# A decode and prompt step with PEER experts on one core: U and V rows in one table, one gather of 8 KB a pick, the gate of each pick on ScalarE

## The chip, the cores and the metric

The kernel runs on one core of a Trainium2 chip. The metric is device time in microseconds of one execution. The engines are TensorE (PE), VectorE (DVE), ScalarE (ACT), GpSimd (POOL) and SyncE (SP); each takes its instructions in the order in which they were written. POOL issues the gathers, SP the other transfers, and all of them share 16 DMA engines. "PEld" is the loading of weights into PE.

## What is computed

One layer on 1024 prompt tokens and 8 sample tokens, width 1024, all in float32: attention in two parallel groups of heads, an output projection, and then PEER, a layer of 16384 experts. Each expert is one row of `peer_u` and one row of `peer_v`. Each token takes 8 heads x 16 = 128 experts:

```python
def peer_ffn(h, w_q, sub_keys, u, v):              # for blocks hc of 128 tokens
    q = (hc @ w_q).reshape(128, PEER_HEADS, 2, 128)
    sc = jnp.einsum('chpd,hpkd->chpk', q, sub_keys)
    s1, i1 = lax.top_k(sc[:, :, 0], 16)
    s2, i2 = lax.top_k(sc[:, :, 1], 16)
    cand = s1[..., :, None] + s2[..., None, :]     # 256 candidates a head
    top_s, pos = lax.top_k(cand, 16)
    eid = take(i1 * N_KEYS + i2, pos)
    gate = jax.nn.softmax(top_s, axis=-1)
    act = jax.nn.gelu(jnp.einsum('cd,chkd->chk', hc, u[eid]))
    return jnp.einsum('chk,chkd->cd', gate * act, v[eid])
```

The rows of U and V must be gathered from memory: 1032 tokens x 128 experts x 8 KB are 1.08 GB.

## The kernel before

**Tiles and picks.** The tokens are cut into tiles of 128 (0 to 7 for the prompt, one more for the eight sample tokens), in groups (0), (1, 2), (3, 4), (5, 6), (7, sample). A pick is one expert for each of the 128 tokens of a tile: 128 picks a prompt tile, 1024 in all, and eight more for the sample tokens (`pick_u`, where 128 partitions hold the 128 experts of one token). A pick has four steps. A gather of 128 rows of U (4 KB each, 512 KB) into a slot of `u_ring` (`fetch_u`, L1429); the dot of each row with its token's hidden row `hb` on DVE (`dot`, L2316); a gather of the V rows into `v_ring` (`fetch_v`, L1434); and the weighing, acc += w * V. The weighing goes either to PE, as a product with a diagonal matrix that ACT makes from the identity (`spread`, L1944; `weigh`, L1703), or to DVE as a multiply and add into `accs` (L2354).

**Sections.** Between dots and weighings stand sections of 16 picks, one head of one tile. When the 16 dots of a section are done, `gelu_arg` on DVE makes the argument of the tanh for 16 columns at once (L2329 to L2334), `tanh` on ACT takes it (L1935), and `gelu_gate` on DVE makes the weights `wv` (L2341). So the V gather of a pick stands LAG = 18 places behind its U gather. `u_ring` has 6 slots (RU), `v_ring` 7 (RV). POOL's order is: for each place, the U gather of pick p, then the V gather of pick p - 18; before each, a wait that the slot's last reader has finished (`ring_slot_free`): `u_used` from the dots, `v_pe` or `v_dve` from the weighings. Before the first pick of a head POOL waits for `r_idx`, the indices that the ranking on DVE gives (L2198).

**Stages and the planner.** All other work (projections, attention, output projection, key scores, ranking) is cut into stages with parts on PE, ACT and DVE. A planner in the kernel's own file (`Planner`) plays the run with an assumed duration for each part, each pick and each gather. It decides which picks are weighed on PE and which on DVE, and writes down the order of each engine; the order is fixed before the run, and only semaphores hold the engines together. Stages that give the indices of a later tile have due places (`deadlines`, with PACE = 2.9 us a pick).

**Weights and keys.** Weights come in pieces of 1 MB (8 KB a partition) into four buffers `wbuf`; two of these take the eight pieces of `w_q` in each group. The sub-keys `keysT` (1 MB) are loaded once. Before a buffer with a piece of `w_q` is filled again, SP waits for `q_mm`, the last product that reads it. Some weights of the first groups are held in the rings until the gathers begin (`HELD`).

**End.** When a tile's picks are done, `final_sum`, `final_squares` (ACT), `final_scale` and `final_rows` add the sum on PE to that on DVE, normalise and store.

## Time and profile before

| | us |
|---|---|
| median of 3 runs | 3447.81 |
| lowest, highest | 3429.58, 3450.52 |
| span of the profiled execution | 3436.9 |
| PE, DVE, ACT, POOL busy | 2499.1, 2605.7, 604.4, 2333.0 |

The span goes from the first instruction to the last of the profiled execution. The PE clock that was granted is 0.849 of full speed on the mean. Busy times of an engine don't count its register, branch and semaphore instructions. A row of the waits names what ended an idle time; "issue" stands for an idle time that ended with no event that the profile shows. The DMA share is the mean busy share of the 16 DMA engines. It counts a packet from its start to its end, so a packet that itself waits counts as busy, and the share can pass 1.

### The profile page before, as it was taken

The numbers are of one execution on the slowest core, as the hardware profiler recorded it, in microseconds if no ns is written. First come the engines' busy times: TensorE is split into PE (matmuls) and PEld (weight loads), VectorE is DVE, ScalarE is ACT, GpSimd is POOL, SyncE is SP. The second block draws the span as 40 slices with busy tenths as digits, with TensorE's granted clock in tenths as the row PEclk, the third lists the DMA queues.
The fourth block names the chain that finished last, engine by engine and source line by source line (L and its number), as shares of the span: only waits on it lengthen the run. The fifth ranks groups of instructions, "written<-read, shape, count | busy, mean of one in ns | idle before, by whom it ended". The sixth has DMA issues, their size and how long they took to land.

```text
span 3436.9 us, 29857 instructions
## 1 busy us (share of the span) xinstructions
PE 2499.1 (73%) x7158; PEld 1274.5 (37%) x7158; DVE 2605.7 (76%) x6416; ACT 604.4 (18%) x1795; POOL 2333.0 (68%) x2076
## 2 busy tenths in 40 slices
PE   7957757888876788877766689977676545766665
PEld 4444335444433444433333344433332211333221
DVE  2268888788878888887867778887866688878754
ACT  1222221112222211211122111121121101111110
POOL 0047665677676777777777677777777676777775
PEclk9978868899866899998877899998887967898878
DMA  7969998999999999999999999999999999999997
GB/s 291 333 260 391 383 346 320 381 398 379 339 342 337 392 403 412 385 389 354 365 359 340 344 398 412 399 383 366 366 352 394 396 373 386 398 404 354 351 367 301
DMA packets 334308, 1257.85 MB, mean 366 GB/s; under 512 B 40736, under 2 KB 43640, under 8 KB 321696
## 3 DMA queue, kind: packets, MB, share of 16 engines
q0 software_dynamic: 298368, 1086.46, 82.8%
q1 hardware_dynamic: 35768, 169.50, 13.0%
q8 instruction: 59, 0.97, 0.1%
q14 instruction: 113, 0.93, 0.1%
HBM read 1247.04 MB, written 43.37 MB: 375 GB/s over the span
## 4 chain that ended last, share of the span: by engine, by line
POOL 30%; issue 17%; DVE 17%; PE 16%; DMA 12%; DVEq 5%; another core or an unknown queue 2%; ACT 1%; SPq 0%; ACTq 0%; POOLq 0%
POOL u_ring L1429 15%; POOL v_ring L1434 14%; DMA v_ring<-in_peer_v,idx 8%; PE acc L1703 7%; DVE u_ring L2316 5%; DVE accs L2354 4%; DMA u_ring<-in_peer_u,idx 3%; DVEq L2353 2%; PE pA L1633 2%; PE pS L1491 2%; PE pS L1610 1%; PE acc L1491 1%; PE pS L1543 1%; DMA wbuf<-in_w_out 1%
## 5 line engine op out<-in xcount | busy, mean ns | idle before, releaser
L1703 PE MATMUL acc<-v_ring,diag 128*128 128x512 f32 x2516 | 1384.2, 692 | 517.8 <-DMA v_ring<-in_peer_v,idx 340.6
L1429 POOL DMA_INDIRECT u_ring<-in_peer_u,idx x1024 | 1147.9, 1121 | 675.9 <-issue 305.2
L1434 POOL DMA_INDIRECT v_ring<-in_peer_v,idx x1024 | 1161.5, 1134 | 400.5 <-issue 287.3
L2316 DVE SCALAR_TENSOR_TENSOR u_ring<-u_ring,hb 128x1024 f32<-128x1024 f32 x1024 | 1235.0, 1220 | 228.9 <-DMA u_ring<-in_peer_u,idx 195.2
L1703 PEld LDWEIGHTS acc<-v_ring,diag 128*128 128x128 f32 x2516 | 514.3, 218 | 1225.5 <-issue 1091.4
L2354 DVE SCALAR_TENSOR_TENSOR accs<-v_ring,wv,accs 128x1024 f32<-128x1024 f32 x395 | 507.3, 1284 | 79.1 <-DMA v_ring<-in_peer_v,idx 29.9
L1944 ACT ACTIVATE diag<-idn,wv 128x128 f32<-128x128 f32 x629 | 233.5, 396 | 872.2 <-PE acc L1703 568.6
L1633 PE MATMUL pA<-T,wbuf 128*128 128x256 f32 (+2 forms) x1280 | 263.4, 363 | 22.2 <-issue 16.1
L1633 PEld LDWEIGHTS pA<-T,wbuf 128*128 128x128 f32 x1280 | 225.1, 208 | 75.6 <-issue 48.9
L1491 PE MATMUL pS<-wbuf,T 128*128 128x512 f32 (+1 forms) x424 | 176.2, 561 | 0.0
L1610 PE MATMUL pS<-wbuf,T 128*128 128x512 f32 (+1 forms) x288 | 136.6, 636 | 18.6 <-issue 13.0
L1586 PE MATMUL pM<-VB,PT 128*128 128x64 f32 x560 | 85.1, 308 | 49.0 <-issue 29.1
L1491 PEld LDWEIGHTS pS<-wbuf,T 128*128 128x128 f32 x424 | 82.5, 197 | 81.9 <-issue 79.2
L2081 DVE CUSTOM_DVE_ANT_0 S<-pS,maskB 128x256 f32<-128x256 f32 (+6 forms) x56 | 46.2, 824 | 86.9 <-PE pM L1550 42.3
L1586 PEld LDWEIGHTS pM<-VB,PT 128*128 128x128 f32 x560 | 83.0, 225 | 72.6 <-issue 48.0
L1543 PE MATMUL pS<-KTB,qT 64*128 64x512 f32 (+3 forms) x160 | 81.6, 630 | 35.9 <-issue 19.4
L1569 PE MATMUL pT<-idn,S 128*128 128x128 f32 x280 | 51.5, 326 | 72.8 <-ACT aden L1817 60.6
L1935 ACT ACTIVATE gl<-gl 128x16 f32<-128x16 f32 (+1 forms) x65 | 13.9, 215 | 472.2 <-DVE gl L2334 331.2
L1815 ACT ACTIVATE S<-S,anm 128x128 f32<-128x128 f32 (+7 forms) x64 | 49.5, 773 | 242.7 <-DVE anm L2088 187.5
L1610 PEld LDWEIGHTS pS<-wbuf,T 128*128 128x128 f32 (+1 forms) x288 | 55.2, 195 | 97.3 <-issue 95.2
L2316 DVE DVE_READ_ACCUMULATOR u_ring<-u_ring,hb 128x1 f32 x1024 | 83.6, 82 | 0.0
L1569 PEld LDWEIGHTS pT<-idn,S 128*128 128x128 f32 x280 | 39.3, 167 | 108.4 <-ACT aden L1817 74.1
(271 smaller groups left out, 2072.6 us busy)
## 6 DMA issues: line engine op xcount, KB each, us to landing
wbuf<-in_w_q SPq DMA_DIRECT2D x40, 1024.0 KB
out_dil_s<-in_cache_dil SPq DMA_DIRECT2D x8, 4092.0 KB
wbuf<-in_w_in SPq DMA_DIRECT2D x26, 1024.0 KB
wbuf<-in_w_out SPq DMA_DIRECT2D x20, 1024.0 KB
u_ring<-in_peer_u,idx POOLq DMA_INDIRECT x1024
v_ring<-in_peer_v,idx POOLq DMA_INDIRECT x1024
T<-in_xT_all SPq DMA_DIRECT2D x8, 512.0 KB, 13.5
accs<-in_x_all SPq DMA_DIRECT2D x8, 512.0 KB
```

The costliest lines, as they stand in the source:

```text
L1429: pool.indirect_dma_start(u_ring[:, entry % RU, :], None, table, bass.IndirectOffsetOnAxis(rows, 0))\
L1434: pool.indirect_dma_start(v_ring[:, entry % RV, :], None, peer_v, bass.IndirectOffsetOnAxis(rows, 0))\
L1491: m = pe.matmul((acc if g == EARLY else pS)[0:R, 512 * (i % 2):512 * (i % 2) + w], xT[t][:, 4 * half + k, :], weights[:, k * w:(k + 1) * w ...
L1543: pe.matmul(pS[:, b0 * P:b1 * P], q[rows, 4 + p, :], KTB[rows, p, b0 * P:b1 * P], start=True, stop=True)
L1569: pe.transpose(pT[:, k * P:(k + 1) * P], S[:, k * P:(k + 1) * P], idn[:, :])
L1586: pe.matmul(pM[:, 0:64], PT[:, k, :], VB[:, k, cols], start=(k == 0), stop=(k == blocks_of(t) - 1))
L1610: m = pe.matmul(pS[0:R, half * 512:(half + 1) * 512], hT[g][:, k, columns(t)], wbuf[:, b, k % 4 * 512:(k % 4 + 1) * 512], start=(k == 0), ...
L1633: m = pe.matmul(pA[:, 0:width_of(GROUPS[g])], wbuf[:, b, k * 256 + i % 2 * P:k * 256 + (i % 2 + 1) * P], hT[g][:, k, :], start=(k == 0), s ...
L1703: m = pe.matmul(acc[0:R, half * 512:(half + 1) * 512], w, v_ring[:, entry % RV, half * 512:(half + 1) * 512], start=first, stop=last, skip ...
L1944: act.activation(diag[:, i % 4, :], idn[:, :], ACT.Copy, scale=wv[:, section % 2, v[1] % TOPK:v[1] % TOPK + 1]).then_inc(d_set, 1)
L2316: dve.scalar_tensor_tensor(row, row, 1.0, hb[:, t % ROWS, :], ALU.mult, ALU.mult, accum_out=dots[:, section % 2, j:j + 1]).then_inc(u_used, 1)
L2354: dve.scalar_tensor_tensor(accs[:, t % ROWS, :], v_ring[:, e % RV, :], wv[:, section % 2, j:j + 1], accs[:, t % ROWS, :], ALU.mult, ALU.ad ...
```

## The change

`peer_u` and `peer_v` are laid side by side in one table `peer_uv` of rows of 8 KB, on the host, before the run. One gather a pick brings both halves into a ring `uv_ring` of seven slots of 8 KB a partition (RING). The slot is freed by the weighing. There is no LAG and there are no sections: after each dot ACT computes that pick's gate alone (`pick_gate`: Square, two copies, tanh with a scale and a bias from memory, Identity with both), and if the pick goes to PE, spreads it to the diagonal. The softmax gates are written with a factor 0.5, and `r_gate` tells ACT of them. For the sample picks the hidden row comes by a second gather into `hb` (`fetch_h`), which from the third on waits for an earlier dot. The keys no longer stay in SBUF: two heads' keys at a time are loaded with that head's piece of `w_q`, 128 KB each, again for every group; for it SP waits for `k_mm` (the key scores) where it waited for `q_mm`. The planner has separate lines for gates, diagonals, weighings, final steps and dots, each with an urgency, and decides PE or DVE for a pick when its gate is done (`share`); its constants are PACE 2.75, GATE 1.35, DMA8 2.55, POOL 1.4, PE_BIAS -2.0.

```diff
-RU, RV = 6, 7
+RING = 7
-LAG = 18
-def pick_v(p):
-    return pick_u(p - LAG) if p >= LAG else None
...
-PACE = 2.9
+LINES = {"PE": ("weigh",), "ACT": ("gate", "diag", "final"), "DVE": ("weigh", "final", "dot")}
+URGENT = {"gate": 0.4, "diag": 0.5, "weigh": 0.6, "final": 0.7, "dot": 1.0}
+PACE = 2.75
+PE_BIAS = -2.0
+GATE = 1.35
+DMA8 = 2.55
+POOL = 1.4
...
-        u_ring = sb("u_ring", [P, RU, D])
-        v_ring = sb("v_ring", [P, RV, D])
+        uv_ring = sb("uv_ring", [P, RING, 2 * D])
-        keysT = sb("keysT", [P, 2 * HEADS, KEYS])
+        keysT = sb("keysT", [P, 2, 2, KEYS])
...
-                        sp.wait_ge(q_mm, 16 * wg + 2 * (wpart + 1))
+                        sp.wait_ge(k_mm, 16 * wg + 2 * (wpart + 1))
...
                     sp.dma_start(wbuf[:, b, :], w_q[:, 2048 * part:2048 * (part + 1)]).then_inc(wt_in[b], 16)
+                    sp.dma_start(keysT[:, b, :, :], keys[:, 2 * part:2 * part + 2, :]).then_inc(keys_in[b], 16)
...
+            def ring_slot_free(entry):
+                if entry < RING:
+                    pool.wait_ge(z_mm, Z_PARTS[HELD[entry], GROUPS[EARLY][-1]])
+                    return
+                last = PICKS[entry - RING]
+                if ON_PE[last]:
+                    pool.wait_ge(v_pe, PE_ORD[last] + 1)
+                else:
+                    pool.wait_ge(v_dve, DVE_ORD[last] + 1)
+            def fetch(entry, rows):
+                ring_slot_free(entry)
+                pool.indirect_dma_start(uv_ring[:, entry % RING, :], None, peer_uv, bass.IndirectOffsetOnAxis(rows, 0))\
+                    .then_inc(uv_in[entry % RING], 16)
+            def fetch_h(r, rows):
+                if r < 2:
+                    pool.wait_ge(f_sq, NT - 1)
+                else:
+                    pool.wait_ge(u_dot, NT * P + r - 1)
+                pool.indirect_dma_start(hb[:, 2 * (r % 2), :], None, h_scr, bass.IndirectOffsetOnAxis(rows, 0))\
+                    .then_inc(sh_in[r % 2], 16)
...
-            def tanh(section):
+            def pick_gate(p):
+                act.wait_ge(u_dot, e + 1)
+                act.activation(cube[:, c], x, ACT.Square, scale=CUBE)
+                copy(line[:, c], x, GELU_C)
...
+                copy(half[:, c], x, g)
+                act.drain()
+                act.activation(bent[:, c], x, ACT.Tanh, scale=cube[:, c], bias=line[:, c])
+                act.drain()
+                act.activation(wv[:, c], bent[:, c], ACT.Identity, scale=half[:, c], bias=half[:, c]).then_inc(g_w, 1)
...
             def spread(p):
-                act.wait_ge(g_w, SECTIONS["f", section] + 1)
+                act.drain()
...
             def weigh(p):
-                v, e = pick_v(p), V_ENTRY[p]
-                dve.wait_ge(v_in[e % RV], 16 * (e // RV + 1))
+                e, t = ENTRY[p], tile_of(pick_u(p))
+                dve.wait_ge(g_w, e + 1)
                 D_()
```

## Rows read from the trace of the kernel before

**Rows 1.** The page: busy time of the engines, and the two large DMA queues
```profile
PE 2499.1 (73%) x7158; PEld 1274.5 (37%) x7158; DVE 2605.7 (76%) x6416; ACT 604.4 (18%) x1795; POOL 2333.0 (68%) x2076
...
q0 software_dynamic: 298368, 1086.46, 82.8%
q1 hardware_dynamic: 35768, 169.50, 13.0%
```
**Rows 2.** POOL's gathers by line: count, duration min/median/max in ns, first and last start
```profile
L1429 POOL DMA_INDIRECT u_ring<-in_peer_u,idx x1024: 932/942/2132, 167.4 to 3352.9; - x171
...
L1434 POOL DMA_INDIRECT v_ring<-in_peer_v,idxT x8: 936/940/1342, 3406.8 to 3416.1; - x8
```
**Rows 3.** POOL's waits: us in total, times, longest
```profile
POOL u_ring L1429 <- issue: 310.1, 972, 2.4
...
POOL u_ring L1429 <- DVE u_ring L2316: 179.9, 65, 12.9
POOL v_ring L1434 <- PE acc L1703: 91.2, 64, 20.9
```
**Rows 4.** Six stretches: length, busy (instructions) per engine, PE clock, DMA share, GB/s
```profile
1400.00:1600.00 200.00, 149.68 (x458) 79.33 (x457) 160.93 (x422) 38.38 (x113) 151.12 (x133) 0.90 0.99 376
1600.00:1800.00 200.00, 142.89 (x414) 72.81 (x413) 155.28 (x356) 42.68 (x127) 148.96 (x136) 0.85 0.96 359
2200.00:2400.00 200.00, 158.71 (x465) 81.57 (x464) 170.64 (x447) 37.80 (x104) 156.54 (x134) 0.91 0.99 376
2400.00:2600.00 200.00, 139.67 (x375) 64.21 (x376) 146.77 (x316) 41.17 (x121) 158.03 (x138) 0.86 0.98 361
3000.00:3200.00 200.00, 132.56 (x392) 65.09 (x390) 164.51 (x445) 28.01 (x93) 148.39 (x137) 0.88 0.98 376
3200.00:3400.00 200.00, 123.90 (x190) 44.43 (x190) 119.18 (x227) 18.72 (x54) 152.76 (x139) 0.79 0.97 365
```
**Rows 5.** Two of five stretches with a DMA share of 1.00 or more
```profile
1200.00:1400.00 200.00, 174.75 (x496) 90.94 (x495) 162.96 (x467) 30.04 (x81) 147.80 (x129) 0.94 1.02 408
...
2600.00:2800.00 200.00, 111.76 (x208) 39.36 (x206) 139.41 (x223) 19.22 (x57) 140.99 (x128) 0.81 1.02 387
```
**Rows 6.** DMA packets of 20 to 25 us (loads), of 2586 to 2600 (gathers)
```profile
DMA packets 289, 2.11 MB, mean 421 GB/s; under 512 B 32, under 2 KB 32, under 8 KB 32
...
DMA packets 1574, 5.74 MB, mean 410 GB/s; under 512 B 175, under 2 KB 175, under 8 KB 1573
```
**Rows 7.** Two of the five other stretches after the first 200 us
```profile
400.00:600.00 200.00, 139.92 (x454) 83.80 (x453) 171.59 (x400) 39.47 (x120) 121.27 (x111) 0.79 0.91 343
...
1000.00:1200.00 200.00, 139.29 (x427) 82.34 (x426) 165.02 (x306) 44.34 (x129) 142.03 (x128) 0.74 0.96 362
```
**Rows 8.** Timeline, DVE, section work: start, us, then the instruction
```profile
2013.66 0.17 DVE L2330 SCALAR_TENSOR_TENSOR gl<-dots,gates 128x16 f32<-128x16 f32 x1
2013.98 0.30 DVE L2332 TENSOR_SCALAR gl<-gl 128x16 f32<-128x16 f32 x1
```
**Rows 9.** Lines of ACT: busy, mean ns, then idle before and its releasers
```profile
L1944 ACT ACTIVATE diag<-idn,wv 128x128 f32<-128x128 f32 x629 | 233.5, 396 | 872.2 <-PE acc L1703 568.6 <-issue 201.3 <-DVE wv L2341 57.4
...
L1817 ACT ACTIVATE aden<-sink,anm 128x1 f32<-128x1 f32 x64 | 17.8, 279 | 0.0
...
L1935 ACT ACTIVATE gl<-gl 128x16 f32<-128x16 f32 x64 | 13.7, 215 | 451.2 <-DVE gl L2334 331.2 <-issue 120.0
```
**Rows 10.** Timeline: the first gather and the first dot
```profile
167.35 1.08 POOL L1429 DMA_INDIRECT u_ring<-in_peer_u,idx  x1 [166.90 <-DVE idx L2198]
...
171.72 1.23 DVE L2316 SCALAR_TENSOR_TENSOR u_ring<-u_ring,hb 128x1024 f32<-128x1024 f32 x1 [4.11 <-DMA u_ring<-in_peer_u,idx]
```
**Rows 11.** The page's groups: DVE's dots and weighings
```profile
L2316 DVE SCALAR_TENSOR_TENSOR u_ring<-u_ring,hb 128x1024 f32<-128x1024 f32 x1024 | 1235.0, 1220 | 228.9 <-DMA u_ring<-in_peer_u,idx 195.2
...
L2354 DVE SCALAR_TENSOR_TENSOR accs<-v_ring,wv,accs 128x1024 f32<-128x1024 f32 x395 | 507.3, 1284 | 79.1 <-DMA v_ring<-in_peer_v,idx 29.9
```
**Rows 12.** Timeline: the four matmuls of one weighing on PE
```profile
2001.91 1.88 PE L1703 MATMUL acc<-v_ring,diag 128*128 128x512 f32 x4
```

More of the change, by code:

```diff
@@ L661, in ready_pick @@
-            return max(self.landed["v", p], gate)
-        return None
-    def load(self, e, p):
-        out = 0.0
-        for kind, q, time in self.picks[e][self.pick[e]:self.pick[e] + 40]:
-            place = q if kind in ("dot", "weigh", "diag") else None
-            if place is not None and place >= p:
-                break
-            if kind == "weigh" and self.on_pe.get(q) != (e == "PE"):
-                continue
-            out += time
-        for n, i, time in self.parts[e][self.base[e]:self.base[e] + 12]:
-            if self.by[n] <= p:
-                out += time
-        return out
+                return max([gate] + [self.ends["weigh", q] for q in older])
@@ L753, in plan @@
             else:
-                kind, p, time = self.picks[e][self.pick[e]]
-                self.pick[e] += 1
+                kind, p, time = self.picks[e, what][self.pick[e, what]]
+                self.pick[e, what] += 1
                 self.ends[kind, p] = at + time + HOP
@@ L759, in plan @@
         assert self.sent == len(self.gathers) and all(self.base[e] == len(self.parts[e]) for e in ENGINES)
-        assert all(self.pick[e] == len(self.picks[e]) for e in ENGINES) or True
         return self.on_pe
     def place(self):
-        for kind, p, _ in self.picks["DVE"][self.pick["DVE"]:]:
-            if kind in ("dot", "weigh"):
-                return p
-        return PLACES
+        n = self.pick["DVE", "dot"]
+        return self.picks["DVE", "dot"][n][1] if n < len(self.picks["DVE", "dot"]) else PLACES
     def engine_order(self, e):
@@ L1954, in _ @@
                 if what != "stage":
-                    {"tanh": tanh, "diag": spread, "fsq": final_squares}[what](s)
+                    {"gate": pick_gate, "diag": spread, "fsq": final_squares}[what](s)
                     continue
```

446 lines of the change are left out of this document (189 added, 257 removed).

## The prediction

> **What bounds the kernel now.** I read the page first, then the stretches of 200 us, then the waits of GpSimd (POOL), then single lines. The page shows no engine full: PE 73%, DVE 76%, POOL 68%, ACT 18%, but the DMA engines carry packets for 82.8% plus 13.0% of the span [rows 1]. That looks like a kernel bound by transfers. The stretches say more. A POOL gather takes 0.94 us at the median [rows 2], and nearly each has 0.3 us before it that waits for nothing visible (310.1 us over 972 times [rows 3]). So in a stretch I add 0.30 us for each POOL instruction to POOL's busy time. In 2400 to 2600 that is 158.03 + 138 x 0.30 = 199.4 of 200 us; in 2200 to 2400 196.7; in 3200 to 3400 194.5; in the other three of [rows 4] about 190. In these 1200 us POOL issues gathers back to back, 817 of them or 408.5 picks, 2.94 us a pick. The rate there is 359 to 376 GB/s (mean 369), although the engines are called 0.96 to 0.99 busy. Elsewhere the same engines move more: 408 GB/s at 1.02 [rows 5], and 410 GB/s in 14 us of gathers alone [rows 6]. So the six stretches are bound by the issue on POOL, with packets drawn out by waiting. Five stretches (600 to 800, 1200 to 1400, 2000 to 2200, 2600 to 3000) have a share of 1.00 or more at 387 to 408 GB/s: bound by DMA, two of them in [rows 5]. The five others (200 to 600, 800 to 1200, 1800 to 2000) have POOL at 152 to 180 us by the same sum, DMA at 0.89 to 0.96, DVE at 150 to 172 [rows 7]: there POOL waits for ring slots that DVE and PE free late (179.9 and 91.2 us in the whole run [rows 3]). The first 167.4 us have no gather at all [rows 2], and the change leaves them as they are.
>
> **Part by part.** The own time of the profiled execution is its span of 3436.9 us; the median of the runs is 3447.8, 11 us above. I sum on the span and add 11 at the end.
>
> (a) Half the POOL gathers go: 1024 + 1024 + 24 become 1032 + 8. If the instruction costs the same for 8 KB rows (the number of rows stays 128), a pick costs POOL 1.24 us instead of 2.48 at the median. Even if it doubles with the bytes (1.88 + 0.30 = 2.18 us), it is below the 2.56 us that 1 MB takes at 410 GB/s. POOL is off the bound either way. What comes next is DMA: I let the six stretches run at 400 GB/s, between 410 (pure gathers) and the 387 of the poorest DMA-bound stretch. 1200 x 369 / 400 = 1107, a gain of 93 us. Bounds: at 387, 56 us; at 410, 120 us; nothing, if 369 is the rate of these transfers after all.
>
> (b) Packets of 8 KB instead of 4 KB. Five us with 8 KB rows alone (a load of weights) ran at 421 GB/s, gathers alone at 410 [rows 6]: 2.6% less time for the gathered bytes, which are about 85% of the traffic. In the 1000 us of the DMA-bound stretches: 1000 x 0.85 x 0.026 = 22 us. Zero, if a row is cut into two packets.
>
> (c) The keys are no longer loaded once but with every head's weights, 40 pieces of 128 KB, 4 MB more. At 410 GB/s that is 10 us of DMA, and 20 if such small pieces move at half that rate, for which no row stands alone. I take +10. The load of the next head's weights also waits now for the key scores (k_mm) and not for the query product (q_mm); what is queued behind that wait on SP is other loads and the stores. The buffer two heads on is needed 8 matmul groups later, so I cost it at nothing; without that cover PE would idle for a copy and a key product, about 1 us, at each of 40 loads.
>
> (d) DVE loses the section work: five instructions of 16 columns per section, one of about 0.3 us and four of 0.17, with a drain of 0.15 between dependent ones [rows 8]: 1.0 us, with the drains about 1.4. x64 that is 63 to 90 us of DVE time, of which 21 to 29 fall in the DVE-bound third of the span. ACT gains a gate for each pick. Its tanh over 16 columns took 215 ns without pointer operands, an instruction on one column with one pointer 279 [rows 9]. The gate is Square and two copies, overlapped by about 0.1 (0.48 us), tanh and Identity (0.28 each, each behind a drain, taken as long as DVE's 0.15): 1.34 us. Lower bound 5 x 0.19 = 0.95, upper 5 x 0.28 + 0.3 = 1.7. The Trainium skill (ScalarE: Activation LUTs, What ACT_TABLE_LOAD costs) gives 186 ns for immediates, about 93 more for each pointer operand and 93 of overlap; by it the gate would be 1.2 us without the drains, so the sum would not move; the 279 of [rows 9] is that rule's figure for one pointer. x1032 is 1383 us: ACT goes from 604 to about 1990 us, 60% of the span. It is not the bound, and the work is not hidden by nature: it is in the chain of every pick, and in front of the copies out of PSUM on which PE waits. With what I cost for this see (e).
>
> (e) The ring. Before, a u row was held from issue to the end of its dot (6 slots), a v row was asked for 18 picks later and held to its weighing (7 slots). Now one slot is held through everything. Shortest life of a slot: an unqueued gather was issued at 167.35 and its dot began at 171.72 [rows 10], 4.37 us; 1.28 us more for the second half of the bytes; the dot 1.22 [rows 11]; the gate 1.34; drain and diag 0.15 + 0.40 [rows 9]; the four matmuls 1.88 [rows 12]; handovers and POOL's own gap about 0.7. Sum 11.3 us by PE. By DVE (weigh 1.28 [rows 11]) 10.2. Seven slots at today's pace, (3416.1 - 167.4) / 1032 = 3.148 us a pick [rows 2], allow a mean life of 22.0 us. So 10 to 12 us may be lost per pick in queues behind stages on DVE, ACT and PE before the ring is slower than today. That cover is real but thinner than before: a u slot had 18.9 us for about 6 us of minimum. I set the loss from this coupling equal to the relief of DVE (21 us), net zero, with bounds of -60 and +150 us.
>
> (f) The end. Sample picks are now gather, row of h, gather, row of h, and from the third h on POOL waits for an earlier dot (u_dot). Before, the last prompt gather of u was at 3352.9 and the last v gather at 3416.1 [rows 2], with 21 us behind it. Now eight sample picks at some 4 us each (a life up to the dot of about 7 us, two in flight) and the chain gate, spread, weigh behind the last: I take +15 us (0 to 25).
>
> Sum: 3436.9 - 93 - 22 + 10 + 0 + 15 = 3347, plus 11: 3358 us.
>
> **A rule that speaks against it.** First the row: 1200 to 1400 moved 408 GB/s [rows 5]. The Trainium skill (DMA: Bandwidth & Descriptors, Specifications) puts the limit of one core on HBM at about 358 GB/s. By it today's mean of the page is already over the limit, and the change would bring nothing: 3448. By the rows a rate over 400 is held for 200 us, so the rule does not bind here; a weaker form of it is rival 3.
>
> **Rivals.**
> 1. The ring binds (slower). The mean life of a slot goes over 22.0 us, because an ACT order fixed in advance lets gates wait behind a copy whose PE product is late, and the weighing, the slot and the next gather wait in turn. For it: today's dots wait 195 us for rows in all, 0.19 us a dot [rows 11], so mostly the row waits for DVE, not DVE for it; all three engines now stand in one chain. Against: 10 us of cover, and DVE and ACT are each under 85%. Price: at a mean of 23 us, 23 / 7 = 3.286 us a pick, 1032 x 3.286 + 167 + 21 + 11 = 3590. It decides from 22.0 us on.
> 2. The engines bind (about the same). POOL's waits vanish, but DVE at 150 to 172 of 200 us and PE at 124 to 159 leave too little; only (b) and a third of (a) come: 3448 - 22 - 31 + 25 = 3420.
> 3. 369 GB/s is what scattered rows give in these stretches, POOL back to back only by chance. Then (a) is zero: 3448 - 22 + 25 = 3451. Against it stand the 410 GB/s of gathers alone, inside such a stretch.
> 4. DMA full throughout. After 200 us some 1200 MB remain; at 405 GB/s 2963 us, 3163 + 15 + 11 = 3189. For it: POOL has room for it. Against: the five stretches bound by engines.
> 5. An 8 KB row is still two transfers: (b) falls away, 3380; inside the range of the forecast.
>
> **Chances.** Forecast with 5: 0.50. Rival 4: 0.10. Rival 1: 0.23. Rival 2: 0.12. Rival 3: 0.05. A change under 1% (34 us) can't be told from none here. Of the forecast nearly all is faster by over 1%, of rival 2 a third: faster 0.61, same 0.15, slower 0.24. The range goes from 3190 (rival 4) to 3530, short of the middle of rival 1; the forecast's own range is 3270 to 3410.
>
> **What would show it.** POOL busy near 1032 x 0.95 to 1.2, about 1000 to 1250 us, its waits now on v_pe and v_dve, not on issue. 8 KB packets in the gather queue, share times time about 2.5% lower. ACT busy near 2000 us (0.95 us a gate would give 1590). In the stretches that were bound by POOL 395 to 410 GB/s; if they stay at 370 with POOL idle, look at who frees the slot: PE or DVE named by POOL for over 500 us is rival 1 or 2, and rival 1 it is if DVE waits for rows and the DMA share falls under 0.9. The forecast is wrong if POOL's mean time for an 8 KB gather is over 2.2 us, or if ACT is named as releaser of weighings for hundreds of us.

## The result, and the profile after

The changed kernel takes 3398.2 us (median of four runs, 3390.6 to 3413.8), the kernel before beside it 3449.2: a ratio of 0.988, 95% interval 0.983 to 0.992. The forecast was 3358 us with a gain of 2.6%; the time lies inside the range, but only about half of the gain came (1.2% by the ratio, 1.5% by the two medians). In four of the five later sessions the kernel before took 3350 to 3357 us, and the changed kernel, run once more in one of them, 3404.1: a ratio of 1.015 (1.010 to 1.019). So in these two sessions the changed kernel keeps its time and the kernel before does not; what that is worth is taken up below.

The page of the changed kernel, with the lines that answer to [rows 1] and the groups that matter:

```profile
PE 2464.4 (72%) x7098; PEld 1267.7 (37%) x7098; DVE 2574.2 (75%) x6105; ACT 1843.8 (54%) x6883; POOL 1300.2 (38%) x1044
...
q0 software_dynamic: 149760, 1086.39, 79.7%
q1 hardware_dynamic: 41384, 173.70, 13.6%
...
L1379 POOL DMA_INDIRECT uv_ring<-in_peer_uv,idx x1024 | 1283.4, 1253 | 2070.4 <-PE acc L1649 1419.8
L1649 PE MATMUL acc<-uv_ring,diag 128*128 128x512 f32 x2456 | 1338.6, 691 | 493.8 <-ACT diag L1699 479.8
...
L1884 ACT ACTIVATE cube<-dots 128x1 f32<-128x1 f32 x1032 | 203.5, 197 | 970.9 <-DVE uv_ring L2283 960.5
...
L1899 ACT ACTIVATE wv<-bent,half 128x1 f32<-128x1 f32 x1032 | 399.0, 387 | 74.4 <-issue 3.5
L1897 ACT ACTIVATE bent<-dots,line,cube 128x1 f32<-128x1 f32 x1032 | 398.8, 386 | 74.1 <-issue 2.8
L1699 ACT ACTIVATE half<-dots,gates 128x1 f32<-128x1 f32 x1024 | 286.6, 280 | 4.0 <-DVE gates L2175 4.0
```

POOL has fallen from 2333 to 1300 us and ACT has risen from 604 to 1844. The gathers are half as many, and one takes 1.25 us on the mean. ACT computes the gates; before a gate it mostly waits for the dot (960.5 us). PE sits idle before its weighings for about as long as before, but for something else: now it waits for the diagonal, and in the kernel before it mostly waited for the V row, by this row of that kernel:

```profile
L1703 PE MATMUL acc<-v_ring,diag 128*128 128x512 f32 x2516 | 1384.2, 692 | 517.8 <-DMA v_ring<-in_peer_v,idx 340.6
```

The gather queue has 149760 packets where it had 298368 [rows 1], for the same bytes: a row of 8 KB is one packet.

The waits of POOL (us in total, times, longest) show what took the place of the issue rows of [rows 3]:

```profile
POOL uv_ring L1379 <- PE acc L1649: 1421.2, 449, 25.8
POOL uv_ring L1379 <- DVE accs L2290: 329.1, 146, 21.2
...
POOL uv_ring L1379 <- issue: 140.6, 434, 5.1
```

Before, 972 of the u gathers followed the one before them at once. Now POOL waits 1750 us for slots that a weighing has to free, 595 times.

The stretches of [rows 4] and [rows 5], one of [rows 7], and 2800 to 3000, of the changed kernel (length, busy and instructions of PE, PEld, DVE, ACT, POOL, PE clock, DMA share, GB/s):

```profile
1200.00:1400.00 200.00, 178.08 (x518) 95.61 (x517) 157.68 (x434) 106.87 (x398) 77.61 (x62) 0.95 0.98 397
1400.00:1600.00 200.00, 148.81 (x460) 78.74 (x458) 168.92 (x421) 121.75 (x453) 82.54 (x70) 0.93 0.99 398
1600.00:1800.00 200.00, 151.02 (x424) 77.01 (x425) 155.32 (x346) 130.42 (x485) 87.08 (x70) 0.82 0.94 372
2200.00:2400.00 200.00, 151.45 (x441) 78.00 (x440) 164.37 (x406) 118.58 (x437) 78.19 (x70) 0.91 0.96 381
2400.00:2600.00 200.00, 142.02 (x406) 69.19 (x407) 150.02 (x321) 128.98 (x472) 80.10 (x69) 0.85 0.93 369
2600.00:2800.00 200.00, 99.41 (x193) 38.42 (x192) 131.70 (x196) 91.43 (x353) 76.87 (x63) 0.76 0.96 369
2800.00:3000.00 200.00, 85.26 (x237) 37.35 (x238) 160.92 (x269) 84.76 (x340) 87.43 (x58) 0.67 0.92 358
3000.00:3200.00 200.00, 139.19 (x418) 71.13 (x416) 161.64 (x415) 106.84 (x422) 80.75 (x68) 0.83 0.93 375
3200.00:3400.00 200.00, 142.49 (x272) 48.15 (x272) 116.63 (x249) 116.43 (x430) 96.22 (x76) 0.92 0.97 392
400.00:600.00 200.00, 132.85 (x413) 80.06 (x414) 170.95 (x375) 111.79 (x425) 80.33 (x56) 0.73 0.90 347
```

With POOL at 38% the DMA share is not higher but lower: in the six stretches of [rows 4] 0.93 to 0.99 where it was 0.96 to 0.99, and in 1200 to 1400 0.98 at 397 GB/s where it was 1.02 at 408.

**A stretch in which everything waits.** POOL's longest wait between 2400 and 2450 us is 12.5 us. Two views of the changed kernel show how it comes about. First the stretches of 2410 to 2423, 2423 to 2436, and four us inside the second (columns as above), then the chain of work that ended last there (start, us, what; "x8" is eight matmuls):

```profile
2410.00:2423.00 13.00, 12.53 (x37) 6.27 (x36) 8.43 (x18) 6.68 (x25) 7.18 (x7) 1.00 0.98 366
2423.00:2436.00 13.00, 7.17 (x24) 4.36 (x24) 12.16 (x23) 10.09 (x41) 0.54 (x2) 0.78 0.66 280
...
2431.80:2435.80 4.00, 3.95 (x5) 1.85 (x6) 3.83 (x7) 3.70 (x15) 0.00 (x0) 0.50 0.03 12
```
```profile
2413.94 8.90 DMA uv_ring<-in_peer_uv,idx
2422.87 1.22 DVE uv_ring L2283
...
2425.25 0.69 DVE onehot L2142
...
2426.01 0.69 DVE onehot L2145
2426.78 0.69 DVE sel L2147
2427.47 1.13 DVE uv_ring L2283
...
2429.65 0.39 ACT wv L1899
...
2430.93 0.39 ACT wv L1899
...
2431.40 0.41 ACT diag L1699
2431.85 6.35 PE acc L1649 x8
...
2438.96 1.41 POOL uv_ring L1379
```

The reader is to see one loop. A row takes 8.9 us to land, while other gathers are under way with it. DVE makes three dots and then has ranking work (the one-hot lines, 2424.1 to 2427.4) before the next two. The slot that POOL waits for is that of the oldest of the seven picks under way, whose dot began at 2420.17 and whose gate ended at 2424.25. Its diagonal was made at 2431.40, 7.15 us later, because ACT's order has the gates of the four picks behind it first, and two of these hang on the dots behind the ranking. PE was idle for 5.8 us for that diagonal, and its granted clock in 2431.8 to 2435.8 is 0.50, that is 1.2 GHz: 0.91 us a matmul, 3.65 us the four of a weighing, where four took 1.88 [rows 12]. All seven slots are held meanwhile, no gather is under way, and the DMA engines carry 12 GB/s at a share of 0.03. In the same 13 us POOL was busy for 10.4 us in the kernel before.

This is the loop at its worst, and not the common case. In the order that the planner gives ACT, 391 of the 614 diagonals have no other gate between them and the gate of their own pick, and 126, 72 and 25 have one, two and three or more; in the trace of after_again (the changed kernel once more) such a diagonal starts on the mean 0.35, 1.8, 3.6 and 5.6 us or more after its gate has ended. Four or more gates stand before a diagonal six times in the run.

**How long a slot is held.** In the trace of after_again the n-th gather, dot, gate and weighing can be matched, since each engine keeps the order of the picks. From the start of its gather to the end of its weighing a slot is held for 20.4 us on the mean, and then stands empty for 1.4 us until POOL fills it again; nearly half of the slots (48%) are filled within 0.35 us. A pick weighed on PE takes 21.0 us: 10.4 until the row has landed, 2.4 until its dot begins, 3.0 until the gate has ended, 3.2 until the weighing begins and 2.3 for the weighing (the first two are means over all picks whose landing the trace has).

### The profile page after: what moved, and what is told of

Read it like the earlier page. It is cut to its first block, busy times and chain, and to the rows that moved or that the text cites. A ratio compares the mean times of both kernels' runs of the same rounds, so it can differ in the third digit from the quotient of the medians.

```text
span 3412.0 us, 34746 instructions
## 1 busy us (share of the span) xinstructions
PE 2464.4 (72%) x7098; PEld 1267.7 (37%) x7098; DVE 2574.2 (75%) x6105; ACT 1843.8 (54%) x6883; POOL 1300.2 (38%) x1044
## 3 DMA queue, kind: packets, MB, share of 16 engines
q0 software_dynamic: 149760, 1086.39, 79.7%
## 4 chain that ended last, share of the span: by engine, by line
DMA 30%; PE 25%; DVE 24%; ACT 6%; issue 6%; DVEq 4%; POOL 3%; ACTq 1%; SPq 1%; POOLq 0%
DMA uv_ring<-in_peer_uv,idx 23%; PE acc L1649 12%; DVE uv_ring L2283 9%; DVE accs L2290 5%; POOL uv_ring L1379 3%; PE pS L1438 3%; DMA o_all<-in_cache_swa 2%; PE pS L1557 2%; PE pA L1580 2%; DMA wbuf<-zS_scr 2%; ACT bent L1897 2%; ACT wv L1899 1%; PE acc L1438 1%; PE pS L1490 1%; ACT diag L1699 1%
## 5 line engine op out<-in xcount | busy, mean ns | idle before, releaser
L1379 POOL DMA_INDIRECT uv_ring<-in_peer_uv,idx x1024 | 1283.4, 1253 | 2070.4 <-PE acc L1649 1419.8
L1649 PE MATMUL acc<-uv_ring,diag 128*128 128x512 f32 x2456 | 1338.6, 691 | 493.8 <-ACT diag L1699 479.8
L2283 DVE SCALAR_TENSOR_TENSOR uv_ring<-uv_ring,hb 128x1024 f32<-128x1024 f32 x1032 | 1238.2, 1221 | 368.3 <-DMA uv_ring<-in_peer_uv,idx 348.6
L1649 PEld LDWEIGHTS acc<-uv_ring,diag 128*128 128x128 f32 x2456 | 507.5, 218 | 1169.2 <-ACT diag L1699 611.4
L1884 ACT ACTIVATE cube<-dots 128x1 f32<-128x1 f32 x1032 | 203.5, 197 | 970.9 <-DVE uv_ring L2283 960.5
L2290 DVE SCALAR_TENSOR_TENSOR accs<-uv_ring,wv,accs 128x1024 f32<-128x1024 f32 x410 | 526.7, 1285 | 63.4 <-ACT wv L1899 24.5
L1899 ACT ACTIVATE wv<-bent,half 128x1 f32<-128x1 f32 x1032 | 399.0, 387 | 74.4 <-issue 3.5
L1897 ACT ACTIVATE bent<-dots,line,cube 128x1 f32<-128x1 f32 x1032 | 398.8, 386 | 74.1 <-issue 2.8
L1699 ACT ACTIVATE half<-dots,gates 128x1 f32<-128x1 f32 x1024 | 286.6, 280 | 4.0 <-DVE gates L2175 4.0
L1699 ACT ACTIVATE line<-dots 128x1 f32<-128x1 f32 x1032 | 193.3, 187 | 0.0
```

What stands on the lines that cost most here:

```text
L1379: pool.indirect_dma_start(uv_ring[:, entry % RING, :], None, peer_uv, bass.IndirectOffsetOnAxis(rows, 0))\
L1649: m = pe.matmul(acc[0:R, side * 512:(side + 1) * 512], w, uv_ring[:, entry % RING, D + side * 512:D + (side + 1) * 512], start=first, stop ...
L1699: return act.activation(out, in_, ACT.Copy, scale=scale)
L1884: act.activation(cube[:, c], x, ACT.Square, scale=CUBE)
L1897: act.activation(bent[:, c], x, ACT.Tanh, scale=cube[:, c], bias=line[:, c])
L1899: act.activation(wv[:, c], bent[:, c], ACT.Identity, scale=half[:, c], bias=half[:, c]).then_inc(g_w, 1)
```

## The experiments

In the table, "this" is the median of the kernel named, "before" that of the kernel before run beside it on the same chip.

| kernel | what is changed in it | this, us | before, us | ratio (95%) |
|---|---|---|---|---|
| ring6 | six slots | 3562.3 | 3349.8 | 1.063 (1.061 to 1.066) |
| ring8_plan7 | eight slots, order of seven, part left out | 3300.8 | 3349.8 | 0.986 (0.983 to 0.989) |
| ring8 | eight slots, order of eight, part left out | 3317.3 | 3349.8 | 0.991 (0.988 to 0.993) |
| split | two gathers of 4 KB a slot | 3579.5 | 3349.8 | 1.069 (1.065 to 1.073) |
| after_again | the changed kernel | 3404.1 | 3356.6 | 1.015 (1.010 to 1.019) |
| ring8_again | ring8_plan7 once more | 3308.6 | 3356.6 | 0.986 (0.980 to 0.991) |
| gate_one | gate of one instruction, GELU left out | 3343.0 | 3356.6 | 0.996 (0.994 to 0.998) |
| keys_once | keys not reloaded | 3392.6 | 3356.6 | 1.011 (1.006 to 1.016) |
| before_look | the kernel before | 3358.3 | 3355.3 | 0.998 (0.995 to 1.001) |
| before_pool | before, one fill a pick on POOL | 3360.3 | 3355.3 | 1.002 (0.999 to 1.005) |
| bias0 | fewer weighings on PE | 3504.5 | 3355.3 | 1.044 (1.038 to 1.050) |
| plan_times | other times in the planner | 3443.6 | 3355.3 | 1.026 (1.020 to 1.031) |
| before_pool2 | two fills, part left out | 3480.9 | 3464.9 | 1.005 (1.002 to 1.008) |
| bias_m4 | more weighings on PE | 3399.7 | 3464.9 | 0.984 (0.981 to 0.989) |
| ring8_ok | eight slots, whole computation | 3318.0 | 3464.9 | 0.960 (0.956 to 0.964) |
| before_pool2b | before, two fills a pick | 3462.6 | 3356.3 | 1.031 (1.028 to 1.034) |
| before_pool4 | before, four fills a pick | 3823.5 | 3356.3 | 1.141 (1.137 to 1.146) |
| ring8_ok_again | ring8_ok once more | 3315.6 | 3356.3 | 0.987 (0.984 to 0.991) |

**Slots.** The edits of ring6 and of ring8_plan7. In ring8_plan7, ring8 and ring8_again the room for the eighth slot comes from small tiles laid over others and from leaving something out: the final gain is the FFN's gain and one mask is part of the other, so two small loads are saved. In ring8_plan7 and ring8_again the order of the work is that of seven slots:

```diff
-RING = 7
+RING = 6
...
-        uv_ring = sb("uv_ring", [P, RING, 2 * D])
+        uv_ring = sb("uv_ring", [P, 7, 2 * D])
```
```diff
-RING = 7
+RING = 8
+PLAN_RING = 7
...
-        for q in range(max(p - RING, 0), p):
+        for q in range(max(p - PLAN_RING, 0), p):
```

> The changed kernel with six slots in place of seven in the ring, planner included. Theory R (the ring binds: a slot is held 21.8 us on the mean, 7 / 21.8 gives the pace of 3.12 us a pick): with six slots part of the life, the queueing for DMA, shrinks, so the pace becomes 3.25 to 3.4 us and the time 3530 to 3700 us. Theory E (PE and DVE bind through their order, slots are spare): under 1% slower than the changed kernel's 3398, so 3400 to 3430.

> The changed kernel with eight slots, each engine's order still the one planned for seven. To make room the final gain is the FFN gain, one mask is part of the other and two small tiles share room, so the outputs are not the reference's; the work is the same. Theory R: one slot more gives 60 to 110 us, 3290 to 3340. Theory E: the order alone holds it, 3385 to 3400. If DMA share rises from 0.94 to 0.97 or more, R.

> As ring8_plan7, but the planner also reckons with eight slots. Theory R: like ring8_plan7 or up to 1% better, since the plan uses the slot. Theory E: within 0.5% of 3398 unless the plan itself is better.

The changed kernel took 3404 us in the next session. Against that one slot less costs 158 us; one slot more gives 95 us in the same session (ring8_again) and 103 across the two. The planner's own use of eight slots is 16 us worse than its order for seven, so the gain is the slot and not the order. The ring binds. Matched as above, the time from one filling of a slot to the next is 19.6, 21.8 and 24.2 us with six, seven and eight slots (ring6, after_again, ring8_again). Of the 2.4 us that the eighth adds, 1.3 go into the landing of the row (9.4, 10.4, 11.7 us on the mean) and 1.1 into its waiting for the dot (1.6, 2.4, 3.5 us).

**Issue.** In split each slot is filled by two gathers of 4 KB, from two tables:

```diff
-                pool.indirect_dma_start(uv_ring[:, entry % RING, :], None, peer_uv, ...)
+                for c, table in enumerate((peer_u, peer_v)):
+                    pool.indirect_dma_start(uv_ring[:, entry % RING, c * D:(c + 1) * D], None, table, ...)
...
-                dve.wait_ge(uv_in[e % RING], 16 * (e // RING + 1))
+                dve.wait_ge(uv_in[e % RING], 32 * (e // RING + 1))
```

> The changed kernel, but each slot is filled by two gathers of 4 KB rows from two tables, one after the other; ring, gate and plan stay. If the issue on POOL was a bound before (my step a) it is one again: a pick costs POOL about 2 x (1.13 + 0.30) = 2.9 us, and the time goes to 3450 or over. With 4 KB packets alone at work (step b) about 50 to 70 us more than 3398. Rival: neither binds under the ring, then within 0.5% of 3398.

It costs 175 us against the changed kernel of the next session. Its waits of POOL:

```profile
POOL uv_ring L1380 <- issue: 574.3, 1881, 0.8
POOL uv_ring L1380 <- PE acc L1650: 387.5, 154, 21.9
```

POOL is back to back for 1881 of 2064 gathers, and waits for PE a quarter as long as in the changed kernel. The one gather a pick is thus what the change gives (fewer issues and larger packets, which split does not tell apart), the single ring what it costs: with the ring and without the one gather the kernel is 6.9% slower than before.

**The changed kernel again, and the chain behind the dot.** after_again is the same program. gate_one keeps one multiplication of dot and gate in place of the five instructions, GELU being left out. keys_once loads the keys for the first group alone, so that later groups read what stands in the buffers:

```diff
-                act.activation(cube[:, c], x, ACT.Square, scale=CUBE)
-                copy(line[:, c], x, GELU_C)
...
-                copy(half[:, c], x, g)
-                act.drain()
-                act.activation(bent[:, c], x, ACT.Tanh, scale=cube[:, c], bias=line[:, c])
-                act.drain()
-                act.activation(wv[:, c], bent[:, c], ACT.Identity, scale=half[:, c], bias=half[:, c]).then_inc(g_w, 1)
+                copy(wv[:, c], x, g).then_inc(g_w, 1)
```
```diff
+                    if g == 0:
                         sp.dma_start(keysT[:, b, :, :], keys[:, 2 * part:2 * part + 2, :]).then_inc(keys_in[b], 16)
```

> The changed kernel itself, beside the others of this call: the chip of the first experiments ran the kernel before in 3350 us instead of 3449, so the ratio of the changed kernel has to be known beside them. Expected 0.985 to 1.005 of the kernel before. If a chip on which the old kernel is faster (DMA less in its way) gains less from the change, nearer 1.0.

> Eight slots with the order planned for seven, once more, beside the changed kernel on one chip. Theory R (the ring binds): 2 to 4% faster than the changed kernel beside it. Theory E (the engines' order binds): within 0.5%.

> The changed kernel with one instruction a pick as gate (the dot times the softmax gate) in place of five with two drains; GELU is left out, the outputs are not the reference's, plan and ring stay. The gate takes 1.4 us of a life of 21.8 us, one instruction about 0.3. Theory R: the life falls by about 1.1 us of 21.8, 5% at most; with the DMA queue growing in turn, 1 to 3% faster. Theory E: 0 to 0.5%. Over 3%: ACT itself was late, and the gate cost more than its own length.

> The changed kernel, keys loaded with the weights of the first group only; later groups score with what is left in the two buffers, so the outputs are not the reference's. 4 MB less to move: my price was 10 us (0.3%), between 0 and 20. If DMA has slack under the ring, nothing.

A gate shorter by 1.1 us gives 61 us, although ACT is busy for 54% of the span only. If the whole of it shortened the time from one filling of a slot to the next, 1.1 / 7 x 1032 = 162 us would come. The matched traces say where the rest goes: from the start of a dot to the end of its gate it is 1.3 us less (1.71 for 2.98), but a row takes 0.4 us longer to land and 0.2 us longer to be taken up, and a pick weighed on DVE waits 1.2 us longer for it, so a slot is held for 20.2 us instead of 20.4 and stands empty for 1.2 instead of 1.4. With the cost of a slot this says that the chain from the row to the free slot sets the pace, and no engine by itself. Keys not reloaded give 11 us.

**Is POOL's issue the bound before?** This is what step (a) rests on. A small fill stands ahead of each v gather of the kernel before; before_pool has one, before_pool2 and before_pool2b have two, before_pool4 has four (shown):

```diff
+                for k in range(4):
+                    if entry or k:
+                        pool.wait_ge(p_idle, 4 * entry + k)
+                    pool.memset(idle[:, :], 0.0).then_inc(p_idle, 1)
                 pool.indirect_dma_start(v_ring[:, entry % RV, :], None, peer_v, ...)
```

> The kernel before, unchanged, for a profile where it takes about 3350 us. In the first trace (3437 us) six stretches of 200 us had POOL back to back at a mean of 1.12 us a gather and 359 to 376 GB/s. If the chip differs in what POOL takes, the mean gather falls to 1.0 us or under here; if it differs in DMA, POOL stays at 1.1 and the mean packet and the rate at full DMA share differ. If both stay, the difference is in PE's clock.

> The kernel before with one small fill (128 x 16) on POOL more before each V gather, 1032 in all, each some 0.1 to 0.3 us with its gap. If POOL's issue bounds the kernel in the six stretches (about 408 of 1032 picks), those lose all of it: 408 x 0.3 to 0.5 us = 120 to 200 us for a fill with gap of 0.3 to 0.5 us, and the others part of it. Rival: DMA bounds and POOL's time is its shadow, then under 30 us.

> The kernel before with two small fills on POOL before each V gather. The trace with one fill showed that 0.12 us of fill and 0.18 us behind it take the place of the 0.30 us gap, so one fill costs POOL nothing; the second adds about 0.31 us to each pick, 320 us of POOL time in all. If POOL's issue bounds the six stretches (some 410 picks of 2.9 us), at least 410 x 0.31 = 127 us more. If the gathers over 0.94 us are long because the DMA engines hold POOL back, they get shorter instead (mean 1.13 to about 1.0 us) and the time rises by under 40 us.

> The kernel before with two small fills on POOL ahead of each V gather and nothing else changed. One fill took the place of the 0.30 us gap that stands between two gathers anyway and moved nothing; in an earlier trace two fills put the V gather 0.45 us behind the U gather in place of 0.30, so the dose is about 0.15 us a pick. If POOL's issue bounds the six stretches (step a: 408 picks), the time rises by 408 x 0.15 = 61 us, ratio about 1.018. If the long gathers there (1.14 us on the mean against 0.94 at the median) are gathers that wait for the queue, the fills are taken out of that waiting: under 12 us, ratio 1.000 to 1.004, and the mean of a gather falls by up to 0.07 us.

> The same with four fills ahead of each V gather: a dose of about 0.45 us a pick. If POOL's issue bounds the six stretches: at least 408 x 0.45 = 184 us more, ratio 1.05 or above, and more than that since POOL would be the bound in other stretches too. If gathers wait for the queue: POOL's own minimum is 2 x (0.94 + 0.30) + 0.45 = 2.93 us a pick, just under the pace of 3.15, so the time rises by under 1.5% (50 us), and the mean of a gather falls from 1.13 toward 1.0 us.

One fill changed nothing that can be told from none (ratio 1.002, 0.999 to 1.005). That looked like an answer against step (a) and was none: the fill (0.13 us) and the 0.18 us behind it took the place of the 0.30 us that stand between two gathers anyway. before_pool2 can't be read: its edit also halved a loop of the input projection, so that it leaves out half of that projection's products, 360 matmuls, and its dose is mixed with a gain. The clean ones are plain: two fills cost 106 us, four 467 us. First the kernel before (before_look), then the one with four fills: POOL by line (busy, mean ns, idle before), of the second also the gather queue, the fills, one stretch and a piece of the timeline:

```profile
L1429 POOL DMA_INDIRECT u_ring<-in_peer_u,idx x1024 | 1161.6, 1134 | 640.2 <-issue 289.1 <-DVE idx L2198 187.6 <-DVE u_ring L2316 163.6
```
```profile
q0 software_dynamic: 298368, 1086.46, 79.3%
...
L1431 POOL DMA_INDIRECT u_ring<-in_peer_u,idx x1024 | 1176.5, 1149 | 520.6 <-issue 308.6 <-DVE idx L2204 190.5 <-DVE u_ring L2322 21.5
...
L1439 POOL MEMSET idle<- 128x16 f32 x4128 | 477.2, 116 | 195.6 <-PE acc L1709 17.4
...
2400.00:2600.00 200.00, 142.19 (x387) 71.60 (x385) 146.60 (x389) 34.04 (x94) 163.78 (x348) 0.84 0.92 325
...
2457.33 0.94 POOL L1431 DMA_INDIRECT u_ring<-in_peer_u,idx  x1 [0.30 <-issue]
2458.26 0.64 POOL L1439 MEMSET idle<- 128x16 f32 x4
2459.05 1.89 POOL L1440 DMA_INDIRECT v_ring<-in_peer_v,idx  x1
```

From the end of a u gather to the v gather there are 0.78 us now and were 0.30: 0.48 x 1024 = 492 us, and 467 come out. Two fills make 0.45 of the 0.30, 154 us, and 106 come out, where the six stretches alone (408 picks) would give 61. So POOL's issue bound more of the kernel before than six stretches, by the small dose some two thirds of it (an estimate, 106 / 154); with the large dose it binds nearly everywhere, but there it is a slower POOL that does. Neither sum is clean, since the gathers grew too: by 42 us in all with two fills and by 98 with four, while POOL's waits for slots fell from 229 us to 110 and 39. Had the gathers been long (1.13 us on the mean, 0.94 at the median) because they waited for a queue, they would have grown shorter; they grew longer (with four fills 1.149 for u, 1.209 for v). The share of the DMA engines is no measure of how full they are: here 325 GB/s stand beside a share of 0.92, and the same 298368 packets take 0.793 x 3810 = 3021 us against 0.828 x 3437 = 2846 in the kernel before.

**The planner.** Its fixed order decides who waits. bias0 sets PE_BIAS to 0 and bias_m4 to -4 (with the change -2: 614 weighings on PE, with 0 463, with -4 731); plan_times gives the planner a gate of 1.5 us and 2.1 us for a weighing on PE:

```diff
-PE_BIAS = -2.0
+PE_BIAS = 0.0
```
```diff
-GATE = 1.35
+GATE = 1.5
...
-            return [("weigh", p, 1.85 if e == "PE" else 1.36) for p in places]
+            return [("weigh", p, 2.1 if e == "PE" else 1.36) for p in places]
```

> The changed kernel planned with PE_BIAS 0 in place of -2: more picks are weighed on DVE. In the changed kernel POOL waited 1421 us for weighings on PE and 329 us for those on DVE, while DVE waited 349 us for rows. If PE is the late releaser, 0.5 to 1.5% faster than 3400; if DVE is as full as PE, the same or slower by 1%.

> The changed kernel planned with PE_BIAS -4, more picks on PE. Bias 0 cost 3%, a longer assumed time on PE 1.3%, so the optimum may lie beyond -2: 0 to 1% faster than 3400. If -2 is the optimum, up to 2% slower.

> The changed kernel planned with a weighing on PE at 2.1 us instead of 1.85 and a gate of 1.5 us instead of 1.35, nearer to what the trace shows. If the order fixed in advance is off because of wrong durations, 0.5 to 2% faster than 3400; else within 0.5%.

bias0 costs 100 us: DVE is busy for 2762 us instead of 2574, and the granted clock of its profile is 0.794 against 0.842. bias_m4 gives nothing (3400 us), although its clock is 0.870: a matmul of a weighing takes 0.66 us on the mean for 0.69, but there are more of them and PE is busy for 2596 us instead of 2464. The times taken nearer to the trace made it worse by 40 us. So the order has weight, but none of these three other orders is better; one that puts diagonals first wasn't tried.

**Eight slots with the whole computation.** ring8_ok finds the eighth slot by laying small tiles over others and by loading the final gain for each tile into the rows of h, which are free by then:

```diff
-        fgain = sb("fgain", [P, D])
...
+            def load_gain(t):
+                i, R = OI[t], rows_of(t)
+                sp.wait_ge(f_sq, i + 1)
+                sp.dma_start(hb[0:R, t % ROWS, :], final_gain.broadcast_to([R, D])).then_inc(fg_in[i % 2], 16)
...
-                dve.scalar_tensor_tensor(accs[0:R, i % ROWS, :], accs[0:R, i % ROWS, :], rsf[0:R, 0:1], fgain[0:R, :],
+                dve.scalar_tensor_tensor(accs[0:R, i % ROWS, :], accs[0:R, i % ROWS, :], rsf[0:R, 0:1], hb[0:R, t % ROWS, :],
```

> The changed kernel with eight slots and all of the computation: the room comes from the final gain, which is now loaded again for each tile into the hidden rows that are no longer needed (4 MB more of DMA, some 11 us), and from small tiles that share room. Order planned for seven slots. The shortened form of it took 3309 us where the kernel before takes 3357; with the loads 3315 to 3335, 0.7 to 1.3% faster than before on that chip.

> The kernel with eight slots and the whole computation, once more, to have its ratio to the kernel before in a second session. It took 3318 us where the kernel before took 3465. If the new kernels keep their time and only the kernel before moves between sessions: 3310 to 3325 us again, a ratio of 0.958 beside 3465 or 0.988 beside 3357. If both move together, the ratio stays at 0.96 whatever the kernel before takes.

It takes 3318 and 3316 us in two sessions, where the kernel before took 3465 and 3356: 4.0% and 1.3% faster. The changed kernel was run in neither of the two; against its 3398 and 3404 us elsewhere ring8_ok is 80 to 88 us faster. The page of ring8_ok_again (queues; issues with KB each and median us to landing) and one stretch:

```profile
q0 software_dynamic: 149760, 1086.39, 80.9%
q1 hardware_dynamic: 42408, 177.40, 14.1%
...
uv_ring<-in_peer_uv,idx POOLq DMA_INDIRECT x1024, 11.7
...
2400.00:2600.00 200.00, 137.69 (x370) 62.05 (x369) 139.53 (x252) 123.11 (x453) 83.05 (x71) 0.87 1.00 397
```

and the issue row of ring6 and of after_again:

```profile
uv_ring<-in_peer_uv,idx POOLq DMA_INDIRECT x1024, 9.2
```
```profile
uv_ring<-in_peer_uv,idx POOLq DMA_INDIRECT x1024, 10.1
```

In 2400 to 2600 it moves 397 GB/s where the kernel before moved 361 [rows 4] and the changed one 369: this is the rate that step (a) asked for, and over the five of the six stretches that lie before its end the mean is 396. But a row also takes 11.7 us to land at the median with eight slots, 10.1 with seven and 9.2 with six: a part of each new slot is spent standing in the DMA queues.

## Why the prediction was wrong

The sum can be set against the trace in the time of the DMA engines (share x span). Before: gathers 0.828 x 3436.9 = 2846 us, other loads and stores 0.130 x 3436.9 = 447, neither 144. After: 0.797 x 3412.0 = 2719, 0.136 x 3412.0 = 464, neither 229. So the span of the profile fell by 25 us: -126 by the gathers, +17 by the rest, +84 of time in neither. This is bookkeeping and not a cause, since the share counts waiting too. Forecast: -115 (steps a and b), +10 (c), +15 (f), and nothing for (e).

**(a) and (b): the cause right, the rates not reached.** That POOL's issue was a bound is shown by before_pool2b and before_pool4, and it bound more of the run than 1200 us. The gathers' time fell by 126 us where 115 were forecast, but that near agreement proves little: the time of the same packets moved by 175 us with POOL's pace alone, and how much of the fall is the larger packet stays open. The rates are the better test. "In the stretches that were bound by POOL 395 to 410 GB/s" did not come: the six stand at 381 on the mean (369 before), worth 39 us of the 93. The five stretches that the prediction called bound by DMA were to gain 22 us by (b) and lost: 381 GB/s on the mean where they had 397, some 42 us (2600 to 2800 fell from 387 to 369, 2800 to 3000 from 393 to 358). The five others went from 350 to 364, some 40 us, for which the prediction had nothing. Where the DMA engines had been fed best, the ring feeds them worse. With eight slots the rate of the six comes.

**(c) right in its size.** keys_once gives 11 us where 10 were forecast. The wait on the key scores, which was costed at nothing, is in no run by itself.

**(d) right.** The gate takes 1.40 us from the start of Square to the end of Identity, which is within the 0.95 to 1.7 and near the 1.34: 0.20 and 0.19 overlapped with 0.28, then 0.386 and 0.387 for the two instructions with two pointers, which I had at 0.28 each, and 0.07 for each drain, which I had at 0.15. The Trainium skill (ScalarE: Activation LUTs, What ACT_TABLE_LOAD costs) has 186 ns and 93 more for each pointer operand, so 372 for two; the rows say 386, and for none and one 187 and 280. ACT is busy for 1844 us where about 1990 were forecast. DVE's relief is smaller than it looks: its busy time fell by 31.5 us only, since 15 more picks are weighed on it (19 us).

**(e) is the step that failed.** "I set the loss from this coupling equal to the relief of DVE (21 us), net zero." The runs showed that the coupling is what binds: POOL waits 1750 us for slots, one slot more gives 95 us, and a gate shorter by 1.1 us gives 61. In the bookkeeping above 84 us more lie in neither kind of transfer; if the 27 of (f) are taken off, some 57 are left for the ring (an estimate). The mechanism was that of rival 1. From one filling of a slot to the next it is 7 x (3389.0 - 167.7) / 1032 = 21.8 us, from these rows of POOL's gathers (first and last start):

```profile
L1379 POOL DMA_INDIRECT uv_ring<-in_peer_uv,idx x1024: 932/1045/2967, 167.7 to 3352.8; - x171
L1379 POOL DMA_INDIRECT uv_ring<-in_peer_uv,idxT x8: 937/938/1382, 3355.8 to 3389.0; - x8
```

This number is seven times the pace, whatever sets the pace, so that it lies just under the 22.0 of the prediction proves nothing; the 22.0 was the same sum for the kernel before. What counts is that a slot is held for 20.4 of the 21.8 us (after_again), where the prediction had 10.2 to 11.3 of work and the rest as cover. The cover was too large on two counts. First, I counted the row's way as 5.65 us, that of a gather that meets no queue [rows 10]; a loaded one takes 10.4 us on the mean in after_again (9.4 with six slots, 11.7 with eight), so nearly 5 us of the cover were gone before any engine was late. That I had wanted the DMA engines full and had priced a transfer as if they were empty is the error. Second, each handing over has its own wait, for which I had 0.7 us in all: a landed row waits 2.4 us for its dot, and from the end of the gate to a weighing on PE it is 3.2 us where I had 0.55. ACT follows a fixed order in which a diagonal can stand behind the gates of later picks (223 of 614), and POOL takes the slots in order, so it waits for the oldest pick. That a weighing can come at 1.2 GHz, in 3.65 us, I did not have at all; but the clock is no new cost of the change, for a matmul of a weighing takes 691 ns on the mean where it took 692. What is new is that it falls into the life of a slot that holds the U row too.

**(f) too small.** From the start of the last prompt pick's last gather to the end of the span it is now 3412.0 - 3352.8 = 59.2 us; before it was 3436.9 - 3404.6 = 32.3, by this row of before:

```profile
L1434 POOL DMA_INDIRECT v_ring<-in_peer_v,idx x1024: 932/942/2246, 219.7 to 3404.6; - x171
```

That is +27 us, just above the bound of 25. The start of the prompt's last gather came 52 us earlier.

**The rivals.** Rival 1 named the mechanism that took the gain, at a price far too high: it had 23 us from one filling to the next, and 21.8 came. Rival 2 (the engines bind) is near in time (3420) and wrong in cause: with the eighth slot the same engines run 2.5% faster with the whole computation (3318 us against 3404), and 2.8% with the order unchanged (ring8_again against after_again). Rival 3 falls with before_pool4 and with the 397 GB/s of the eight slots. Rival 4 didn't come: the share in the changed kernel is 93.3%. Rival 5 is out by the packets: 149760 where there were 298368. The rule of the Trainium skill (DMA: Bandwidth & Descriptors, Specifications), a limit of some 358 GB/s on HBM, is not borne out: the changed kernel holds 397 GB/s for 200 us, and by the rule its time would be that of before.

**What stays open.** The kernel before takes 3350 to 3357 us in some sessions and 3449 to 3465 in others, the new ones 3398 and 3404 (seven slots) and 3318 and 3316 (eight) in one session of each kind. So whether the change gains 1.2% or loses 1.5% depends on the session; my forecast was made against the slower one. It is not simply the chip: the one numbered 2 had the kernel before at 3357 us in one session and at 3465 in another. In the two profiled executions of the kernel before (spans 3436.9 and 3364.0) POOL's gathers have nearly the same means (1.121 and 1.134 us, 1.134 and 1.128). What differs is POOL's wait for slots and for what the trace can't name: 293.7 us, that is 179.9 and 91.2 [rows 3] and the row below, against 229.4 in before_look:

```profile
POOL v_ring L1434 <- remote: 22.3, 18, 5.5
```
```profile
POOL u_ring L1429 <- DVE u_ring L2316: 163.6, 73, 6.3
POOL v_ring L1434 <- PE acc L1703: 65.8, 76, 20.9
```

That places 64 of the 73 us but does not say why; no run told it apart. The time is lost where the prediction had POOL waiting for slots: the five stretches of 200 to 600, 800 to 1200 and 1800 to 2000 have 350 GB/s on the mean in the slower execution and 368 in before_look, while the five at a full DMA share have 397 and 398. Against before_look the bookkeeping of the changed kernel's second profile (after_again) reads -119 by the gathers, +19 by the rest and +137 in neither: the transfers gain the same, and the ring takes more than all of it.

## What to carry to other kernels

When two rings become one, price the life of a slot with the latency of a loaded queue, and not with that of the first transfer: the better the plan fills the DMA engines, the longer each row takes to land, and the ring must be deep enough for both. Here the landing of a row took 10.4 us and not 5.65, which makes the 11.3 us of the prediction 16 (an estimate) of the 21.8 between two fillings of a slot, and one slot more was the difference between -1.2% and -4.0% against the slower kernel before, and between +1.5% and -1.3% against the faster: look for that slot before the change is judged. To find out whether an issuing engine is the bound, put small instructions in front of its transfers, but more than its gap can hide.

## What the runs showed of the hardware

- A gather of 128 rows costs POOL nearly the same for 8 KB rows as for 4 KB: 0.93 us at the least for both, 1.05 and 0.94 at the median, 1.25 and 1.13 on the mean, and 0.30 us to the next one. One small fill (128 x 16, 0.13 us) fits into these 0.30 us for nothing.
- The share of the DMA engines in the records includes time in which they wait: 325 GB/s at 0.92 with a slow issuer, 397 at 0.98 with a quick one.
- A gather of 1 MB takes longer to land the more of them are asked for: 9.4, 10.4 and 11.7 us on the mean with six, seven and eight slots.
- TensorE, idle for 5.8 us for a diagonal, stood at 1.2 GHz (granted clock 0.50) in the four us after, and a weighing took 3.65 us for 1.88 just when the ring waited for it. With 463 weighings on PE instead of 614 the mean clock was 0.794, with 731 it was 0.870.
